# Low-rank norms spread over the value tiles, query rotations under the third weight block, lambda first

## What is computed

```python
def even_mixer(hn, p, ctx, layer_idx):
    proj = hn @ p['w_in']                        # 1024 -> 3*512 + 192 + 128 + 32 columns
    qa, ka, va, q_down, ckv, kpe = jnp.split(proj, [...], axis=-1)
    ...
    qb = heads(rmsnorm(q_down, p['q_norm']) @ p['w_uq'], HB)
    ckv = rmsnorm(ckv, p['kv_norm'])             # the two low-rank norms
    if latent:                                   # rotations of queries, keys and kpe
        q1, q2, k1, k2 = rope_2d(q1, ta), rope_2d(q2, ta), rope_2d(k1, ta), rope_2d(k2, ta)
        q_pe, kpe = rope_2d(q_pe, tb), rope_2d(kpe, tb)
    ...
    lam = (jnp.exp(jnp.sum(lambda_q1 * lambda_k1)) - jnp.exp(jnp.sum(lambda_q2 * lambda_k2)) + lambda_init)
    oa = attend(q1, k1a, v_all, sa) - lam * attend(q2, k2a, v_all, sa)
```

## Time and profile before

| | |
|---|---|
| median of 3 runs | 2162.46 us (2159.67 to 2165.41) |
| profiled execution, device time | 2163.41 us |
| its span in the trace | 2161.6 us |
| TensorE busy | 94% of the span |
| VectorE, ScalarE, GpSimd busy | 51%, 31%, 7% |
| mean granted TensorE clock | 0.965 of full speed |

### The profile page before, as it was taken

The page is one execution under the profiler, slowest core; times in us unless marked ns, Lnnn a source line. Parts: engine busy times, 40 slices in busy tenths (PEclk is TensorE's granted clock), DMA queues, the critical chain, the costliest instruction groups (busy, mean ns, idle before and its releaser), DMA issues.

```text
span 2161.6 us, 41220 instructions
## 1 busy us (share of the span) xinstructions
PE 2035.3 (94%) x18352; PEld 1763.6 (82%) x18352; DVE 1103.9 (51%) x1990; ACT 674.7 (31%) x1214; POOL 152.6 (7%) x145
## 2 busy tenths in 40 slices
PE   5997999999999999989998789999989999999998
PEld 3784444579999999989995378888956999999997
DVE  3225733256555562354545756877754655556323
ACT  3212534133333341232334424333212433324211
POOL 2000000000000000000003623222100000000000
PEclk7998989999999999999998879999999999999999
DMA  9023718222222212321210000000021222222222
GB/s 337 28 79 125 276 40 297 92 79 79 79 79 73 65 52 64 81 91 60 79 49 9 18 2 3 3 3 3 3 83 40 79 79 79 79 79 54 61 74 76
DMA packets 141505, 163.72 MB, mean 76 GB/s; under 512 B 2368, under 2 KB 106864, under 8 KB 141328
## 3 DMA queue, kind: packets, MB, share of 16 engines
q1 hardware_dynamic: 137872, 148.81, 21.1%
q0 software_dynamic: 3456, 12.28, 1.6%
HBM read 157.32 MB, written 3.75 MB: 75 GB/s over the span
## 4 chain that ended last, share of the span: by engine, by line
PE 85%; DVE 9%; DMA 2%; ACT 2%; issue 1%; POOL 0%; ACTq 0%; SPq 0%; DVEq 0%; POOLq 0%
PE ps L220 80%; DMA ring<-in_ada_w 1%; PE ps L1721 1%; DVE small L1244 1%; DVE work L2262 1%; DMA ring<-in_ffn_up 1%; PE ps L1137 1%; DVE work L490 1%; PE ps L341 1%; ACT work L1194 0%; DVE x_lo_r L496 0%; DMA ring<-in_l_w_out 0%; DVE work L2307 0%; PE ps L2039 0%; PE ps L2021 0%
## 5 line engine op out<-in xcount | busy, mean ns | idle before, releaser
L220 PE MATMUL ps<-x_hi_r,w_lo 128*128 128x320 f32 (+3 forms) x2240 | 520.9, 307 | 3.8 <-ACTq L204 2.8
L220 PE MATMUL ps<-x_lo_r,w_hi 128*128 128x320 f32 (+2 forms) x1664 | 391.8, 309 | 8.2 <-DVE g_lo L765 8.2
L220 PE MATMUL ps<-work 64*64 64x64 f32 (+7 forms) x4942 | 361.2, 269 | 38.0 <-ACT work L2182 9.1
L220 PE MATMUL ps<-x_hi_r,w_hi 128*128 128x320 f32 (+2 forms) x1664 | 394.9, 311 | 0.9 <-issue 0.9
L220 PEld LDWEIGHTS ps<-x_hi_r,w_lo 128*128 128x128 f32 (+1 forms) x2240 | 373.1, 187 | 5.9 <-ACTq L204 3.0
L220 PEld LDWEIGHTS ps<-work 64*64 64x64 f32 (+4 forms) x4942 | 234.0, 148 | 148.1 <-issue 90.0
L220 PEld LDWEIGHTS ps<-x_lo_r,w_hi 128*128 128x128 f32 x1664 | 284.5, 189 | 8.8 <-DVE g_lo L765 8.7
L220 PEld LDWEIGHTS ps<-x_hi_r,w_hi 128*128 128x128 f32 x1664 | 281.1, 188 | 1.4 <-issue 1.3
L596 DVE SCALAR_TENSOR_TENSOR work<-ps,par,work 128x511 f32<-128x511 f32 (+1 forms) x188 | 103.3, 549 | 268.2 <-ACT work L730 260.6
L643 DVE TENSOR_TENSOR w_lo<-ring,w_hi 128x1024 fp32r<-128x1024 f32 (+1 forms) x152 | 158.4, 1077 | 96.5 <-ACT w_hi L632 96.5
L730 ACT ACTIVATE work<-ps,par 128x640 f32<-128x640 f32 x88 | 77.9, 886 | 397.9 <-PE ps L220 397.9
(11 more groups left out here) (348 smaller groups left out, 2449.1 us busy)
## 6 DMA issues: line engine op xcount, KB each, us to landing
ring<-in_ada_w SPq DMA_DIRECT2D x24, 2048.0 KB, 7.9
ring<-in_ffn_up SPq DMA_DIRECT2D x44, 1024.0 KB, 7.0
ring<-in_ffn_down SPq DMA_DIRECT2D x16, 1408.0 KB, 6.8
ring<-in_l_w_in SPq DMA_DIRECT2D x11, 1024.0 KB, 5.1
ring<-in_l_w_out SPq DMA_DIRECT2D x4, 2048.0 KB, 9.0
ring<-in_l_w_in SPq DMA_DIRECT2D x3, 2048.0 KB, 9.0
h<-in_xT POOLq DMA_DIRECT2D x1, 2560.0 KB, 14.6
out_yT<-work POOLq DMA_DIRECT2D x2, 768.0 KB, 4.0
```

Of the source, the lines that this page charges most:

```text
L220: return pe.matmul(out, lhsT, rhs, start=first, stop=last)
```

## The change

The helpers' three `stats_` functions go. Their steps for the two norms are written out in the three queues, one at a time: the sums of norm 0 behind value tile 0, its turning behind tile 1, the sums of norm 1 behind tile 2, its turning behind tile 3. The four query rotations move under the third weight block, one behind each of its units, with banks 6 and 7; keys and kpe follow behind tiles 0 to 2. VectorE's order is interleaved accordingly, with the last value weights' low parts between rotations 0, 1 and 2. Lambda's product becomes VectorE's first step, its sum goes behind tile 2 (into bank 5) and its exponential behind ScalarE's copy of tile 3. The wait for the constants' loads (`m0_loaded`) moves ahead of the first query rotation.

```diff
-        def stats_act(act, planned):
...
-        def stats_pe(pe, planned):
...
-        def stats_dve(dve, planned, ch):
...
+        ROT_BANK = (6, 7, 6, 7, 1, 3, 1, 3, 1)
+
+        def rotated(pe, m):
+
+            if m >= 2:
+                pe.wait_ge(sg("m0_roped"), m - 1)
+            if m < 8:
+                mm(pe, bank(ROT_BANK[m]), rotA[:, :], q(m, 0, NL) if m < 4 else kk_(m - 4, 0, NL)).then_inc(sg("m0_rot"), 1)
+            else:
+                mm(pe, bank(ROT_BANK[m], 512, 0, QK), rotB[0:QK, 0:QK], kpe_b[0:QK, 0:NL]).then_inc(sg("m0_rot"), 1)
+
+        def low_sums(pe, k):
+            srcs, mat = low_norms[2][k][0:2]
+            if k >= 1:
+                pe.wait_ge(sg("st_used"), k)
+            else:
+                pe.wait_ge(sg("m0_roped"), 4)
+            for j, (src, kk, *_) in enumerate(srcs):
+                c = 2 * k + j
+                pe.wait_ge(sg("st_sq"), c + 1)
+                token_sums(pe, 3, sqb[0:kk, (c % 2) * NT:(c % 2) * NT + NT], mat[0:kk, :], j == 0, j == len(srcs) - 1)\
+                    .then_inc(sg("st_sum"), 1)
+
+        def low_turn(pe, k):
+            pe.wait_ge(sg("st_rep"), k + 1)
+            turn_back(pe, 3, k % 2).then_inc(sg("st_turned"), 1)
...
+                    if j == 2:
+                        if i == 0:
+                            pe.wait_ge(sg("m0_loaded"), 16 * 16)
+                        rotated(pe, i)
...
                 if tt == 0:
-                    pe.wait_ge(sg("m0_loaded"), 16 * 16)
                     pe.wait_ge(sg("m0_copied"), V0)
-                if tt == 2:
-                    stats_pe(pe, low_norms)
...
+                    low_sums(pe, 0)
+                    rotated(pe, 4)
+                    rotated(pe, 5)
+                elif tt == 1:
+                    low_turn(pe, 0)
+                    rotated(pe, 6)
+                    rotated(pe, 7)
+                elif tt == 2:
+                    low_sums(pe, 1)
+                    rotated(pe, 8)
+                    pe.wait_ge(sg("lam_prod"), 1)
+                    mm(pe, bank(5, 2), ones[0:64, :], small[0:64, 26:28]).then_inc(sg("lam_sum"), 1)
+                elif tt == 3:
+                    low_turn(pe, 1)
             released.append((sg("m0_prod"), n))
-            pe.wait_ge(sg("lam_prod"), 1)
-            mm(pe, bank(6, 2), ones[0:64, :], small[0:64, 26:28]).then_inc(sg("lam_sum"), 1)
...
-            stats_act(act, low_norms)
...
+            squares(0)
             for tt in range(5):
                 act.wait_ge(sg("m0_prod"), n + 1)
                 slot = tt if tt < 4 else 5
                 act.activation(v_b[:, 512 * slot:512 * slot + 512], bank(2 * (n % 3)), ACT.Copy).then_inc(sg("m0_copied"), 1)
                 n += 1
-            act.wait_ge(sg("lam_sum"), 1)
-            act.activation(small[:, 28:30], bank(6, 2), ACT.Exp).then_inc(sg("lam_exp"), 1)
+                if tt == 0:
+                    low_root(0)
+                    squares(1)
+                elif tt == 2:
+                    low_root(1)
+                elif tt == 3:
+                    act.wait_ge(sg("lam_sum"), 1)
+                    act.activation(small[:, 28:30], bank(5, 2), ACT.Exp).then_inc(sg("lam_exp"), 1)
 
         def mix0_dve(dve, ch):
+            lp = par[0:64, PC["lam"]:PC["lam"] + 4].rearrange("p (a b) -> p a b", b=2)
+            dve.tensor_tensor(small[0:64, 26:28], lp[:, :, 0], lp[:, :, 1], ALU.mult).then_inc(sg("lam_prod"), 1)
...
-            for j in (2, 3):
-                for part in range(4):
-                    m0_w_lo(dve, j, part)
-            for m in range(9):
...
+            for part in range(4):
+                m0_w_lo(dve, 2, part)
...
+            roped(0)
+            m0_w_lo(dve, 3, 0)
+            m0_w_lo(dve, 3, 1)
+            roped(1)
+            m0_w_lo(dve, 3, 2)
+            m0_w_lo(dve, 3, 3)
+            roped(2)
+            roped(3)
+            roped(4)
+            low_spread(0)
+            roped(5)
+            low_scale(0)
+            roped(6)
+            roped(7)
+            low_spread(1)
+            roped(8)
+            low_scale(1)
+            dve.wait_ge(sg("st_used"), 2)
```

More of the change, by code:

```diff
@@ L961, in mix0_pe @@
                 wh, wl = m0_k3(m0_hi[j][:, :]), m0_k3(m0_lo(j))
-                for c0, c1 in cuts:
+                for i, (c0, c1) in enumerate(cuts):
                     pe.wait_ge(sg("m0_copied"), n - 2)
@@ L1045, in mix0_act, with squares, low_root @@
             act.wait_ge(sg("m0_copied"), V0)
-            stats_act(act, low_norms)
+            def squares(k):
+                for j, (src, kk, *_) in enumerate(low_norms[2][k][0]):
+                    c = 2 * k + j
+                    if c >= 2:
+                        act.wait_ge(sg("st_sum"), c - 1)
+                    for piece, a, b in src.pieces if src is ckv_new else ((src, 0, NT),):
+                        ins = act.activation(sqb[0:kk, (c % 2) * NT + a:(c % 2) * NT + b], piece, ACT.Square)
+                    ins.then_inc(sg("st_sq"), 1)
+            def low_root(k):
+                _, mat, scale, eps, _ = low_norms[2][k]
+                act.wait_ge(sg("st_sum"), 2 + k)
+                act.activation(root(k, 1), bank(6, NCH), ACT.Sqrt, bias=small[:, eps:eps + 1], scale=scale).then_inc(sg("st_root"), 1)
+            squares(0)
             for tt in range(5):
@@ L1061, in mix0_dve, with roped @@
                 dve.tensor_tensor(xl(t), hn(t), xh(t).bitcast(F32), ALU.subtract).then_inc(sg("x_lo"), 1)
-            for j in (2, 3):
-                for part in range(4):
-                    m0_w_lo(dve, j, part)
-            for m in range(9):
+            for part in range(4):
+                m0_w_lo(dve, 2, part)
+            def roped(m):
                 dve.wait_ge(sg("m0_rot"), m + 1)
@@ L1068, in mix0_dve, with low_spread, low_scale @@
                     src = q(m, 0, NL) if m < 4 else kk_(m - 4, 0, NL)
-                    rope(dve, src, src, bank(1 + 2 * (m % 2)), cosA, sinA, ch, done=sg("m0_roped"))
+                    rope(dve, src, src, bank(ROT_BANK[m]), cosA, sinA, ch, done=sg("m0_roped"))
                 else:
                     x = kpe_b[64:QK, 0:NL]
-                    rope(dve, x, x, bank(1, 512, 64, QK), cosB, sinB, ch, 64, QK, done=sg("m0_roped"))
+                    rope(dve, x, x, bank(ROT_BANK[m], 512, 64, QK), cosB, sinB, ch, 64, QK, done=sg("m0_roped"))
                 dve.wait_ge(sg("m0_roped"), m + 1)
[L1074 to L1077, removed]
+            def low_spread(k):
+                dve.wait_ge(sg("st_root"), k + 1)
+                ch(dve.reciprocal(root(k, 1), root(k, 1)))
+                spread(dve, k, k % 2, 1).then_inc(sg("st_rep"), 1)
+            def low_scale(k):
+                outs = low_norms[2][k][4]
+                dve.wait_ge(sg("st_turned"), k + 1)
+                for j, (out, in_, gain, kk) in enumerate(outs):
+                    for piece, a, b in out.pieces if out is ckv_new else ((out, 0, NT),):
+                        ins = dve.scalar_tensor_tensor(piece, piece, gain, pair_ap(3, a, b, 0, kk), ALU.mult, ALU.mult)
+                ins.then_inc(sg("st_used"), 1)
+            roped(0)
[16 more added lines that the diff above has]
+            dve.wait_ge(sg("st_used"), 2)
             lam_init = 0.8 - 0.6 * math.exp(0.0)
```

## The result

| | before | changed |
|---|---|---|
| median of 12 runs | 2163.58 us (2159.2 to 2167.24) | 2152.86 us (2147.1 to 2159.46) |
| profiled execution, device time | 2163.41 us | 2148.49 us |
| its span | 2161.6 us | 2146.7 us |
| TensorE busy | 94% | 95% |
| mean granted clock | 0.965 | 0.973 |

The ratio is 0.9947, with a 95% interval of 0.9934 to 0.9960: 8.7 to 14.3 us faster. The forecast was 2149.5, with a range from 2145 to 2155.5.

A forecast was written before the change was run, and what follows sets the result against it. The prediction took TensorE, busy 94% of the span, as the bound, with stalls at the norms and the tail. Attention 12.3 us earlier plus 1.2 for faster first scores made 13.5, forecasting 2149.5 us, range 2145 to 2155.5.

The forecast's parts named there:

- The two stalls: TensorE waits at the low-rank norms behind value tile 2 and in the tail before attention; both to be covered.
- every spare: Slack of the other engines' queues against TensorE's new order; the smallest was 2.5 us, at rotation 7.
- The path: TensorE from the third block's end to attention's first matmul: 41.5 us instead of 53.80, so attention 12.3 us earlier.
- turnings: Two groups of five transposes between value tiles, 0.77 us each, 1.54 together, upper bound 2.7.
- lambda's sum: Two records of two columns on TensorE, taken as 0.2 us, between 0 and 0.40.
- The first scores: Attention's first scores, 2.55 us at 1.2 GHz before, would run at 2.4 GHz: another 1.2 us gained.
- The rival of the clock: The clock falls at the inserted sums or turnings, 2.4 us a fall; one fall gives 2151.9; one or two falls 0.13.
- main branch: The forecast itself, chance 0.70: 13.5 us gained, granted clock reading 1.00 from 60 to 200.
- The rule of the Trainium skill: Transposes do not count as busy for the clock, so the two turnings would lose 2.4 us each, some 2154.
- The block load: Attention's second modulation block, loaded into tile 4's slot, lands in 7.8 to 8.9 us; spare 1.2, 1 lost if late.
- Slower: Clock falls at the first sums and stays low until attention: 26.5 us more, 2176; chance 0.03.
- no effect: A wait still holds TensorE at an insert; the whole old stall back would be 2162; chance 0.02.

The follow-up runs named there:

- norms_alone: The kernel before with only the two norms spread over the value tiles, rotations and lambda in their old places; 2156.4 us against 2166.02, ratio 0.996.
- after_again: The changed kernel, unchanged, for a second trace; stage 100.4 us, span 2152.7 us.
- lam_last: The changed kernel with lambda's product, sum and exponential put back behind value tile 4; stage 102.7 us, span 2158.0 us.
- after_third: The changed kernel, unchanged, on a third occasion, timed in five rounds against the kernel before; 2151.57 us against 2166.0, ratio 0.9942.
- before_again: The kernel before, unchanged, for a second trace; stage 112.3 us, span 2165.8 us.

## Why the prediction was right

**The two stalls.** Both went where the steps said, and no wait took their place: every spare worked out for the stage was enough. Norm 0's sums, for one, ended at 151.37 (worked out: 151.6). The first turning stood at 160.45 instead of 158.9: the 1.8 us of clock, less the 0.2 by which it was ahead. The split between the two is where the forecast was high. By its terms the norms are worth 9.4 us (12.0 from tile 2's end to the next rotation, less the 4.9 of sums and turnings that stay, and 2.3 of slow clock) and the rest 4.1. norms_alone has 9.2; the rest gave 1.9 to 3.3 in the stage, and nothing that can be told behind attention.

**The path.** I had 41.5 us for it, and attention 12.3 us earlier. Measured from the first unit's copy to the first scores it is 64.13 (119.15 to 183.28) instead of 74.69: 10.6 us, and 12.4 without the 1.8 of the slow stretch. The terms:
- single rotations 0.85 (0.86 taken), tiles 5.57 (5.54), first sums 2.21 (2.23), second 1.01 (1.15);
- turnings 0.55 (0.77; that was the length of a busy interval, which overlaps the next matmul), but the stretches behind the first sums and the first turning are each 0.2 longer in after_again than the 7.26 worked out;
- lambda's sum was mis-sized. Rotation 8, the sum and tile 3 are 7.00 in after_again; rotation 8 and tile 3 in lam_last are 6.50. That is 0.5 us on TensorE, where I took 0.2 and at most 0.4;
- copy and hand-over behind tile 4: 0.7 (0.9 taken).

Chain of after_again from the first rotations behind the sums, and of lam_last over tile 3:

```profile
149.57 7.46 PE ps L220 x28
157.04 0.55 PE ps L356 x5
157.58 7.45 PE ps L220 x28
165.04 1.01 PE ps L341 x10
166.04 7.00 PE ps L220 x28
```

```profile
168.33 6.50 PE ps L220 x26
```

**The first scores** took 1.40 us: the 1.2 came, and norms_alone and lam_last show what they cost with a tail in front (2.55 and 2.19).

**The rival of the clock** was right in kind, and the forecast's main branch, a granted clock of 1.00 from 60 to 200, was not. The rival had 0.13 for one or two falls at a price of 2.4; a fall came in two of three traces of the changed kernel, at 1.4 and 1.6 in the stage (100.4 against 101.8 and 102.0). The price was too high because it was taken from 4.8 us of slow work behind the norms. The fall here lasted from about 152.6 to 156.1, and no longer. The profiled execution's stage gain of 11.7 lies between my forecast's 13.5 and the 11.1 of one fall. That the number came out well in spite of the dip is owed in part to this small price, which I had not worked out. The step that was too light is the one that set twenty records in 2.23 us against "2.8 us and more" of thin records in the other place and took them for safe. By the share of 0.61 in the earlier trace rows the clock there fell at about 293.2, so it was 2.6 us, and the margin was thinner still. The rule of the Trainium skill ("TensorE: Matmul & The Clock Gate", "Part 4: PE-mode transpose"), by which the turnings would be the risk, is not borne out: none of the 20 turnings between tiles, in ten traces, has a slow stretch that begins behind it. All falls among the tiles stand at the one-column sums.

**The block load** came later than I had bounded. Issued at tile 4's end, 182.6, it landed in 10.0 us, above the 7.8 to 8.9 of the earlier trace rows; the same load took 7.9 before. I had said that the four output stores shared the same stretch before, but there GpSimd issued the first of them 4.9 us behind the load (189.6 and 194.45), and here 0.9 us behind it (183.53). The other traces bear it out: with the first store 0.9 us behind it, this load took 9.8 to 10.7 us, in ten traces; with 3.0 to 5.0 us between, 7.8 to 8.0, in four. The rows of the changed kernel: landing of the ring's loads from 178 to 250, and the wait for them from 180 to 260.

```profile
DMA to landing us min/median/max: 7.8/7.9/10.0
```

```profile
PEld ps L220 <- DMA ring<-in_ada_w: 0.2, 1, 0.2
```

My spare of 1.2 us was used up to the last, at a cost of 0.2 here, none in after_again and after_third, and 0.6 to 1.2 in the three traces with doubled sums.

**Slower, and no effect**, are excluded by the chain and by the interval of the time.

**What is missing.** The forecast gain was 13.5, the medians are 10.7 apart. Of the 2.8 between, 2.0 are in the stage, whose gain is 11.5 in the means: about 1.0 is the fall of 1.5 in two of three traces, 0.3 lambda's sum, and 0.6 the first trace of before, in which the slow clock behind the norms lasted longer than in before_again. In before_again rotations and tile 3 behind the norms take 178.27 - 169.96 = 8.31 us, not the 9.61 of the earlier trace rows:

```profile
169.96 2.74 PE L220 MATMUL ps<-work 128*128 128x512 f32 x4
...
178.27 1.88 PE L220 MATMUL ps<-work 128*128 128x512 f32 x4
```

The last 0.8 are within the interval. All this is a sum by the stage's means; at attention's end its smaller terms can no longer be told apart.

## What to carry to other kernels

Spread a serial chain of small steps over long independent work: it cost nothing here but its own TensorE time and, in some executions, a dip of the clock of about 1.5 us, once each queue's spare was worked out from rows. Take away the larger stall first, and test the smaller one by itself: the tail looked like 4.8 us on the chain, gave 1.9 to 3.3 in the stage, and gave no time that these runs can tell from none. And price a stage against two traces of the kernel before, from an anchor ahead of the change, and read it once more at the end of the next stage: one trace had the stage 1.2 us longer than the next, and the end of the program moved by 4 us with clock dips that the change had no part in.

## What the runs showed of the hardware

A busy TensorE can lose its clock. Behind twenty one-column records in 2.2 us, with wide matmuls right behind them, the clock fell to 1.2 GHz in two of five traces; with forty it fell in three of three, one of them with a full-width matmul of 512 columns in the middle. Such a fall cost 1.4 to 1.6 us of stage time, or 3.3 with forty. A 2 MB load landed in 9.8 to 10.7 us when 0.6 MB of stores began 0.9 us behind it, and in 7.8 to 8.0 when they began 3.0 us or more behind it.
